# One step of a hybrid encoder on one Trainium2 core: the prompt's down projection by seven products of halves, its weight sums made in DRAM by accumulating DMAs

## What is computed

```python
def hybrid_layer(x, ...):
    h = rmsnorm(x, norm_mix_g)
    ...
    x = x + jnp.concatenate([y_a, y_b, y_c], axis=-1) @ w_mix_out
    h = rmsnorm(x, norm_mem_g)
    ...
    x = x + om @ w_mo
    h = rmsnorm(x, norm_ffn_g)
    gt, ffn_buf_new = causal_dwconv(h @ w_gate, ffn_buf, ffn_conv_w)
    x = x + (jax.nn.silu(gt) * (h @ w_up)) @ w_down      # 640x2816 @ 2816x1024
```

## Time and profile of the kernel before

| What | Value |
|---|---|
| three executions | 944.78, 945.42, 945.74 us |
| profiled execution, first to last instruction | 943.7 us |
| PE, matmuls | 931.8 us busy (99%), x6919 |
| PE, weight loads | 841.9 us (89%) |
| DVE | 648.3 us (69%) |
| ACT | 452.1 us (48%) |
| POOL | 170.0 us (18%) |
| DMA | 103.70 MB, queue q1 32.6% of 16 engines |

### The profile page before, as it was taken

How to read it: one execution, slowest core, us unless ns; L and a number is a source line. 1 busy time by engine, 2 the same in 40 slices (tenths; PEclk the granted TensorE clock), 3 DMA queues, 4 the chain that set the end, 5 groups by cost and what they waited for, 6 DMA issues and landing times.

```text
span 943.7 us, 16891 instructions
## 1 busy us (share of the span) xinstructions
PE 931.8 (99%) x6919; PEld 841.9 (89%) x6919; DVE 648.3 (69%) x1083; ACT 452.1 (48%) x836; POOL 170.0 (18%) x198
## 2 busy tenths in 40 slices
PE   9999999999999999999999999999999999999998
PEld 7899888998889877799888999999999999888886
DVE  7627888777775565552666999999999999435321
ACT  6634454648566454554654445444444445333310
POOL 0071101103664331000002032222222220000000
PEclk9999999999999999999999999999999999999999
DMA  8624142121104084244904322222222224412221
GB/s 303 225 88 145 54 168 93 47 94 49 45 5 135 2 290 154 82 142 157 317 18 138 113 87 90 90 90 90 88 73 74 79 89 152 147 64 93 78 89 56
DMA packets 73820, 103.70 MB, mean 110 GB/s; under 512 B 2576, under 2 KB 53904, under 8 KB 73360
## 3 DMA queue, kind: packets, MB, share of 16 engines
q1 hardware_dynamic: 73744, 102.63, 32.6%
HBM read 92.27 MB, written 10.35 MB: 109 GB/s over the span
## 4 chain that ended last, share of the span: by engine, by line
PE 51%; DVE 3%; ACT 2%; POOL 1%; issue 1%; ACTq 0%; POOLq 0%; DVEq 0%
PE bank L1222 8%; PE bank L1220 8%; PE bank L1221 8%; PE bank L538 5%; PE bank L537 5%; PE bank L536 5%; PE bank L484 2%; PE bank L486 1%; PE bank L485 1%; PE bank L466 1%; PE bank L562 1%; PE bank L1034 1%; PE bank L564 1%; PE bank L563 1%; PE bank L1036 1%
## 5 line engine op out<-in xcount | busy, mean ns | idle before, releaser
L2168 DVE TENSOR_TENSOR wlo<-wraw,whi 128x2048 fp32r<-128x2048 f32 (+1 forms) x56 | 126.2, 2253 | 102.2 <-ACT whi L1617 93.0
L1617 ACT ACTIVATE whi<-wraw 128x2048 fp32r<-128x2048 f32 (+1 forms) x58 | 109.3, 1885 | 101.9 <-PE bank L538 72.8
L498 PE MATMUL bank<-hhi,whi 128*128 128x320 f32 x352 | 116.4, 331 | 0.6 <-issue 0.6
L500 PE MATMUL bank<-hhi,wlo 128*128 128x320 f32 x352 | 108.7, 309 | 0.0
L499 PE MATMUL bank<-hlo,whi 128*128 128x320 f32 x352 | 108.7, 309 | 0.0
L498 PEld LDWEIGHTS bank<-hhi,whi 128*128 128x128 f32 x352 | 66.2, 188 | 5.0 <-issue 3.6
L499 PEld LDWEIGHTS bank<-hlo,whi 128*128 128x128 f32 x352 | 66.2, 188 | 3.0 <-issue 2.4
L500 PEld LDWEIGHTS bank<-hhi,wlo 128*128 128x128 f32 x352 | 66.1, 188 | 0.0
L536 PE MATMUL bank<-whi,hhi 128*128 128x512 f32 x150 | 58.4, 389 | 0.0
L537 PE MATMUL bank<-wlo,hhi 128*128 128x512 f32 x150 | 58.4, 389 | 0.0
L538 PE MATMUL bank<-whi,hlo 128*128 128x512 f32 x150 | 58.3, 389 | 0.0
(11 more groups left out here) (491 smaller groups left out, 2690.4 us busy)
## 6 DMA issues: line engine op xcount, KB each, us to landing
wraw<-in_w_in SPq DMA_DIRECT2D x13, 1024.0 KB, 5.5
wraw<-in_w_gate SPq DMA_DIRECT2D x11, 1024.0 KB, 5.2
wraw<-in_w_up SPq DMA_DIRECT2D x11, 1024.0 KB, 5.1
wraw<-in_w_down SPq DMA_DIRECT2D x10, 1024.0 KB, 5.1
kTs<-in_cache_sb_k SPq DMA_DIRECT2D x8, 512.0 KB, 4.4
vraw<-in_cache_sb_v SPq DMA_DIRECT2D x8, 512.0 KB, 4.9
wraw<-in_w_mix_out SPq DMA_DIRECT2D x4, 1024.0 KB, 6.3
kmT<-in_cache_mem_k SPq DMA_DIRECT2D x8, 512.0 KB, 6.2
```

Of the source, the lines that this page charges most:

```text
L498: T.matmul(o, wh[:, k, cs], hhi[:, k, hs], start=(k == 0), stop=False)
L500: ins = T.matmul(o, wl[:, k, cs], hhi[:, k, hs], start=False, stop=(k == KD - 1))
L1617: V(wv(whi, i), wv(wraw, i), ACT.Copy).then_inc(s["w_hi_ready"], 1)
L2168: V.tensor_tensor(wv(wlo, i), wv(wraw, i), wv(whi, i).bitcast(F32), ALU.subtract)\
```

## The change

The 512 prompt rows, the 2,816 features and the 1,024 columns of the last product are each split in two. Instead of eight products of halves there are seven; the 128 sample rows keep their plain product. Seven products need sums of act halves (four per pair of feature tiles, made by DVE, or by POOL for the first two pairs) and sums of weight halves: t1 = w00 + w01, t3 = w01 + w11, t2 = w00 + t3, t4 = w10 + t2 (the first index is the feature half, the second the column half). POOL issues 16 copies from DRAM to DRAM for their first terms and 16 accumulating DMAs for the additions, each of 352 rows of 512 values (704 KB). PE runs 11 steps with p1, the samples, p3 and p5, then 11 with p6, p7, p4 and p2.

```diff
-FIRST = 3
-LEAD = 2
...
+        for n in range(2 * HF):                        # HF = 11: pairs of rows f and 11 + f of w_down
+            blocks.append((A["w_down"].rearrange("(a f p) c -> f p a c", a=2, p=P)[n % HF], 2, D_MODEL))
...
+        BY_POOL = 2
+        QUARTER_PARTS = 4
+        t1_sum = nc.dram_tensor("first_weight_sum", (ROWS, 512), F32).ap()
+        t_sums = nc.dram_tensor("weight_sums", (ROWS, 3, 512), F32).ap()
...
 PE
-            down("dn", 0, B_DN[0], left_a, NT, ready_a)
-            down("dn", 1, B_DN[1], left_a, NT, ready_a)
+            for i in range(HF):
+                pe.wait_ge(s["parts_lo"], i + 1)
+                lo_cut(pe, B_DN[i])
+                product("p1", i, dn_parts(i, 0), dn_weights(i, 0, 0))      # 2 tiles x 3 matmuls
+                samples(i)                                                 # 2 x 2 x 3 matmuls
+                pe.wait_ge(s["sums_lo"], i + 1)
+                product("p3", i, dn_parts(i, 512), dn_weights(i, 1, 1))
+                pe.wait_ge(s["t1_lo"], i + 1)
+                ins = product("p5", i, dn_parts(i, 256), (t1_hi[t1_slot(i)][:, :], t1_lo[t1_slot(i)][:, :]))
...
+            SECOND = (("p6", 0, 1, 0), ("p7", 256, 1, 1), ("p4", 768, 0, 1), ("p2", 512, 0, 0))
+            for i in range(HF - 2):
+                d = HF + i
+                pe.wait_ge(s["parts_lo"], d + 1)
+                lo_cut(pe, B_DN[d])
+                for name, p0, a, c in SECOND:
+                    ins = product(name, i, dn_parts(d, p0), dn_weights(d, a, c))
+                step(ins, B_DN[d])
+            for name, p0, a, c in SECOND:
+                for t in range(2):
+                    for i in (HF - 2, HF - 1):
...
 SP
+            load_t1(0)
+            load_t1(1)
+            for d in range(2, 2 * HF):
+                if d == 4:
+                    passed(sp, B_DN[0])
+                    passed(sp, gu_block("up", FT // 2 - 1))
                     sp.wait_ge(s["rows_kept"], 16)
                     D(xres[:, :, :], kept).then_inc(s["rows_back"], 16)
+                load_w(B_DN[d])          # waits for PE's step d-4; from d = 11 two DMAs, 768 KB of t_sums and 256 KB of w_down
+                if d < HF:
+                    load_t1(d)           # 256 KB, waits for PE's step d-3
...
+            for name, t0, c0 in (("p6", 0, 512), ("p7", 2, 512), ("p4", 2, 0), ("p2", 0, 0)):
+                for t in range(2):
+                    evacuated(sp, (name, t))
+                    D(O["y_prompt"][(t0 + t) * P:(t0 + t + 1) * P, c0:c0 + 512], xres[:, t0 + t, c0:c0 + 512])\
+                        .then_inc(s["out_y"], 16)
...
 POOL
+            def copy_quarter(t, a, c, q):
+                G.dma_start(sum_rows(t, q), quarter_rows(a, c, q)).then_inc(s["weight_rows"], 16)
+            def add_quarter(t, q, source):
+                G.dma_start(sum_rows(t, q), source, accum_op=ALU.add).then_inc(s["weight_rows"], 16)
...
-            for n in past:
+            for x, n in enumerate(past):
                 evacuated(pool, ("z", n, 0))
...
                 ins.then_inc(s["past_ready"], 1)
+                copy_quarter(*copies[x])
...
                 G.tensor_tensor(vmask[h % 2][:, :, :], ...).then_inc(s["vm_ready"], 1)
+            pool.wait_ge(s["weight_rows"], 16 * len(copies))
+            for q in range(QUARTER_PARTS):
+                add_quarter(1, q, quarter_rows(0, 1, q))
+                add_quarter(3, q, quarter_rows(1, 1, q))
             for n, f in enumerate(GN):
                 if n == 0:
                     filled(pool, ("oT", 0))
                 pool.wait_ge(s["yhi_ready"], n + 1)
                 G.tensor_tensor(mxlo[:, f, :], mixed(f), mxhi[:, f, :].bitcast(F32), ALU.subtract)\
                     .then_inc(s["ylo_ready"], 1)
+            pool.wait_ge(s["weight_rows"], 16 * 6 * QUARTER_PARTS)
+            for q in range(QUARTER_PARTS):
+                add_quarter(2, q, sum_rows(3, q))
             passed(pool, B_MV[1])
             for n in range(2):
                 ins = G.memset(pz[n][:, :, :, :], 0.0)
             ins.then_inc(s["pz_ready"], 1)
+            pool.wait_ge(s["weight_rows"], 16 * 7 * QUARTER_PARTS)
+            for q in range(QUARTER_PARTS):
+                add_quarter(4, q, sum_rows(2, q))
...
+            for m in range(BY_POOL):     # the four act sums of 256 columns of pairs 0 and 1
...
 ACT
+            cut_sums(0)
+            for d in range(1, 2 * HF):
+                cut_parts(d)             # 256 + 256 columns in pass one, 1,024 in pass two
+                cut_hi(B_DN[d])          # 2,048
+                if 1 < d <= HF:
+                    cut_sums(d - 1)      # 512
+                if d < HF:
+                    cut_t1(d)            # 512
+                if d == HF:
+                    keep_product("p1", sum_p1)
+                if d == HF + 1:
+                    keep_product("p5", sum_p5)
...
 DVE
+            sums_lo(0)
+            t1_low(0)
+            for d in range(1, 2 * HF):
+                if BY_POOL <= d < HF:
+                    first_sum(d)         # 256 columns each of the four sums
+                parts_lo(d)
+                if BY_POOL <= d < HF:
+                    third_sum(d)
+                if 1 < d <= HF:
+                    sums_lo(d - 1)
+                cut_lo(B_DN[d])
+                if BY_POOL <= d < HF:
+                    second_sum(d)
+                if d < HF:
+                    t1_low(d)
+                if BY_POOL <= d < HF:
+                    fourth_sum(d)
+                if d == HF:
+                    first_rows()         # four additions to xres from banks
+                if HF + 3 <= d < HF + 8:
+                    kept_rows(d - HF - 3)
+            last_rows()                  # 14 more additions of 512 columns from the banks of p6, p7, p4, p2
```

More of the change, by code:

```diff
@@ L1254, in _, with product @@
                         across((kind, j), gu_block(kind, j), hhi, hlo)
[L1255 to L1259, removed]
-            down("dn", 0, B_DN[0], left_a, NT, ready_a)
-            down("dn", 1, B_DN[1], left_a, NT, ready_a)
+            def product(name, i, stationary, moving, ts=(0, 1), first=0, last=HF - 1):
+                for t in ts:
+                    c = slice(stationary[2] + t * P, stationary[2] + t * P + P)
+                    hi, lo = stationary[0][:, c], stationary[1][:, c]
+                    if i == first:
+                        take((name, t))
+                    o = bank[use[name, t][0]][:, :]
+                    T.matmul(o, hi, moving[0], start=(i == first), stop=False)
+                    T.matmul(o, hi, moving[1], start=False, stop=False)
+                    ins = T.matmul(o, lo, moving[0], start=False, stop=(i == last))
+                    if i == last:
+                        done(ins, (name, t))
+                return ins
@@ new lines, in dn_parts, with dn_weights, samples @@
+            def dn_parts(m, c):
+                hi, lo = part_hi[part_slot(m)], part_lo[part_slot(m)]
+                return hi, lo, c
+            def dn_weights(d, a, c):
+                cs = slice(512 * c, 512 * c + 512)
+                return wv(whi, B_DN[d])[:, a, cs], wv(wlo, B_DN[d])[:, a, cs]
+            def samples(i):
+                hi, lo = part_hi[part_slot(i)], part_lo[part_slot(i)]
+                for c in range(2):
+                    if i == 0:
+                        take(("cs", c))
+                    o = bank[use["cs", c][0]][:, :]
+                    for a in range(2):
+                        ss = slice(768 + a * P, 768 + a * P + P)
+                        wh, wl = dn_weights(i, a, c)
+                        T.matmul(o, hi[:, ss], wh, start=(i == 0 and a == 0), stop=False)
+                        T.matmul(o, hi[:, ss], wl, start=False, stop=False)
+                        ins = T.matmul(o, lo[:, ss], wh, start=False, stop=(i == HF - 1 and a == 1))
+                    if i == HF - 1:
+                        done(ins, ("cs", c))
@@ L2811, in _ @@
                 if j == FT // 2 - 1:
-                    for n in range(LEAD):
-                        act_lo(n)
+                    parts_lo(0)
                 if j in SEVEN["up"]:
@@ new lines, in kept_rows @@
+            def kept_rows(n):
+                if n == 0:
+                    for name in ("p1", "p3", "p5"):
+                        for t in range(2):
+                            evacuated(dve, (name, t))
+                    link(V.tensor_tensor(sum_p5[:, :, :], sum_p5[:, :, :], sum_p1[:, :, :], ALU.subtract))
+                    return
+                a, c = divmod(n - 1, 2)
+                x = xres[:, 2 * a:2 * a + 2, 512 * c:512 * c + 512]
+                link(V.tensor_tensor(x, x, (sum_p1, sum_p5)[c][:, :, :], ALU.add))
```

291 lines of the change are left out of this document (224 added, 67 removed).

## The result

Four runs of the changed kernel gave 983.28 to 985.83 us, median 984.47; four of the kernel before on the same chip 944.78 to 945.74, median 945.19. The ratio is 1.0416 (95% interval 1.0403 to 1.0429): 39.3 us slower, where 14.6 were forecast. The profiled execution took 983.28 us with a span of 981.3, 37.6 more than before.

A forecast was written before the change was run, and what follows sets the result against it. PE's own stream was taken to set the time nearly everywhere. The profiled span of 943.7 less 15.0 plus a 29.2 us stall gave 957.9, with 1.7 around it 959.6, said as 960 us; range 929 to 984.

The forecast's parts named there:

- PE's own saving: Down projection: 594 matmuls instead of 660 at 0.2267 us each, so 15.0 us go, all on the path.
- DVE, ACT, loads, start and end of the new stage at 0: New down stage: vector work, loads, first steps and last additions stay covered by PE's matmuls; cost 0, loads at worst 2 us.
- (C): New down stage starves: DVE needs 7.5 us a step instead of 6.8 in pass one, 8 us more; chance 0.05 with (A).
- (D): New down stage: 594 matmuls cost more apiece from scattered tiles; at 0.25 us nothing is left of 15 us; chance 0.02.
- The 16 copies at 0: Behind the selects of attention items: up to about 2 us a copy is covered; cost 0, held till landing up to 3.
- The other eight adds at 0: Four behind the last `mxlo`, four behind `pz`: about 20 us of each POOL gap if held one by one, cost 0.
- The first eight adds: Between last `vmask` product and first `mxlo`: each add held until the one before lands, 33.4 us, PE stalls 29.2.
- a cover: Before the output projection: POOL's first `mxlo` ends at 329.2, PE uses it at 333.36, so 4.2 us of delay are free.
- my own upper bound: Adds before the first `mxlo`, priced by rows that write and read DRAM: 8.2 us each, 58.2 in all, stall 54.0.
- The clock at 0: PE's granted clock after a long wait: 1.00 in every stretch before, a lower one would add a term taken as 0.
- Rival (B): Adds before the first `mxlo`: two under way at a time, pairs landing in 5.6 us, stall 13.4, 943.8 us; chance 0.12.
- Rival (A): Adds before the first `mxlo`: POOL pays only for issuing, stall 2.0, 932.4 us, 930 to 938 with small terms; chance 0.33.

The follow-up runs named there:

- the two profiled runs without the stall: Changed kernel with its first eight adds moved behind the last `mxlo`, 931.67 us; changed kernel without copies and adds, loading `w_down` rows instead, 930.43 us.
- two ahead: Changed kernel with two of the first eight adds before the first `mxlo` and six behind the last: 941.3 us, ratio 0.9951 to the kernel before.
- one ahead: Changed kernel with one of the first eight adds before the first `mxlo` and seven behind the last: 931.1 us, ratio 0.9839 to the kernel before.
- the run with 4,096 bytes: Only eight copies and eight adds on POOL, zeros stored beside them, descriptor store 4,096 instead of 1,024 bytes: all eight adds left in 43 us instead of 54.
- all adds behind: Changed kernel with the first eight adds moved from before the first `mxlo` to behind the last: 931.67 us, ratio 0.9851 to the kernel before.

## Why the prediction was wrong, and where it was right

**PE's own saving: right.** 66 matmuls at 0.2267 are 15.0 us; the trace says 14.96, and the two profiled runs without the stall are 14.9 below the span of before.

**DVE, ACT, loads, start and end of the new stage at 0: right.** No wait of PE inside the stage. DVE was 85% busy in pass one where 91% was worked out. (C) and (D) did not come about.

**The 16 copies at 0: right for PE, incomplete for POOL.** An issue took 0.60 to 0.81 us. Three close ones were more than fits: the third stood 4.7 us at 80.7 to 85.4. I had put the worst at up to 3 us for the closest two. PE waited for none.

**The other eight adds at 0: right.** They stand in POOL's gaps.

**The first eight adds: the failed step.** The mechanism was the forecast one: held one by one, one wait of PE, a cover that came out as 3.7 instead of 4.2 us (56.8 less 53.1; with two ahead 8.4 less 4.6); 0.4 of that is the first `mxlo`, which lasts 1.93 us behind an add (one ahead) instead of 1.53. One ahead is free. The size was not. The term was 7 x 4.7 + 0.8 = 33.4 us with 4.7 read off plain loads into SBUF; it measured 7 x 8.0 + 0.6 = 56.8. A read, a second read and a write are not a load: my own upper bound, made from the rows that write and read DRAM, said 8.2, and the stall of 53.1 lies at its 54.0 and not near 29.2. The text had between its ends "the row that it is nearest to", and a transfer that reads two operands from DRAM and writes one back is nearest to those rows. Taken there, the sum is 943.7 - 15.0 + 54.0 = 982.7 for the span, where 981.3 was measured.

**The clock at 0: a small miss.** It was left "to be looked at". It fell during the long wait, was still at the lower level for the first seven matmuls, and cost 1.3 us; another 1.1 us wait vanished, so that the sum hid it.

**Rival (B), two at a time, was priced wrong.** It gave pairs of adds 5.6 us. By the slope that it used, that is 1,408 KB, the reads of one add; a pair reads 2,816 KB, 7.5 us. Pairs of half the size took 7 to 8, and the two pairs of full adds in the run with 4,096 bytes landed 11.2 and 10.6 us after the first had left. An estimate from these is 3 x 11 + 1 = 34 us, a stall of 30 and not 13.4: two at a time would have cost the change its gain as well. **Rival (A)** was refuted at 1,024 bytes and is what POOL does at 16,384.

What stays open: how much room an add takes exactly (three at most were in flight at 4,096 bytes, one at 1,024), and why the room of a group returns in one piece. The full kernel was not tried with a larger store; its own tiles begin at byte 1,152 and would have to move.

## What to carry to other kernels

A DMA that POOL issues stands in POOL's order and can hold what is behind it: look for the first thing there that the critical engine needs, and place the DMA where POOL has a gap as long as the landings, not as the issues. Here the same eight adds cost 53 us more in one place than in another, 37 us later, where all 32 copies and adds together cost about 1. Price a DRAM to DRAM add by the rows that read and write DRAM, not by loads; and count any new wait of PE with the slow matmuls that follow it.

## What the runs showed of the hardware that was not expected

- An accumulating DMA of 704 KB within DRAM takes 7.5 us alone with one in flight and 4.1 with eight in flight (32.9 us for all). Other traffic adds little on average beside loads, 8.0 us ahead of `mxlo` and 9.1 behind it, but single ones left up to 13.5 us before the next (two ahead), and one beside the stores of zeros took 13.2.
- Issuing costs POOL 0.6 us for a copy and about 0.6 to 0.95 for an add, as long as there is room (with 16,384 bytes the starts of the adds stay 0.59 apart, while their recorded lengths grow from 0.96 to 3.52). The Trainium skill, page "DMA: Bandwidth & Descriptors", section on SWDGE, HWDGE and iDMA, places these descriptors in rings in SBUF. The runs agree in that a larger store, and nothing else, freed POOL: one add in flight at 1,024 bytes, up to three at 4,096, eight at 16,384. The prediction's estimate, room for one or two adds in 1,024 bytes, came out at its lower end: one add, or two copies, or two adds of half the rows. Four times the room gave three adds and not four or more.
- Two copies leave together, and the next two leave together only when both have landed (pairs 7.3 to 8.2 us apart by themselves with 1,024 bytes; the first of a pair lands 5.0 to 6.0 us after it left, the second 6.2 to 7.3), so two in flight do not make a steady stream.
- A wait of PE of 4.6 us, and in one place one of 1.95 us shortly behind one of 1.44, was followed by seven or so matmuls at 1.2 GHz pace (granted clock 0.50 to 0.59), 1.5 us each time; the wait of 53 us cost no more than that. The same wait of 1.44 us was followed by no fall in the kernel before, nor with all adds behind, where the next one was 0.76 (granted clock 1.00 from 397 to 430 us).
